# A decoder's second layer: gate logits by seven half-block products for eight, one weight unit a group

## The reference, cut to what matters

```python
h = _modulate(x, norm1[l], sh1, sc1)
q_a, k_a, v_a, q_b, k_b, v_b, q_n, k_n, v_n, gate_l = jnp.split(h @ w_in[l], IN_OFFSETS, axis=-1)
...
def _merge(outs, gate_logits, w_branch, w_out):
    g = jax.nn.sigmoid(gate_logits.astype(jnp.float32)).astype(gate_logits.dtype)
    g = g.reshape(*g.shape[:-1], N_BRANCHES, D_MODEL)
    y = g[..., 0, :] * (outs[0] @ w_branch[0])
    for n in range(1, N_BRANCHES):
        y = y + g[..., n, :] * (outs[n] @ w_branch[n])
    return y @ w_out
...
x = x + g1 * _merge((o_a, o_b, o_n), gate_l, w_branch[l], w_out[l])
```

## Time and profile before

| | us |
|---|---|
| runs | 1591.43, 1591.34, 1588.87 (median 1591.34) |
| profiled execution | 1588.37 |
| its span, first to last instruction | 1586.7 |
| PE busy | 1533.8 (97%) |
| PEld busy | 832.6 (52%) |
| DVE busy | 700.8 (44%) |
| ACT busy | 365.5 (23%) |
| POOL busy | 129.7 (8%) |

### The profile page before, as it was taken

How to read it: one execution, slowest core, us unless ns; L and a number is a source line. 1 busy time by engine, 2 the same in 40 slices (tenths; PEclk the granted TensorE clock), 3 DMA queues, 4 the chain that set the end, 5 groups by cost and what they waited for, 6 DMA issues and landing times.

```text
span 1586.7 us, 17758 instructions
## 1 busy us (share of the span) xinstructions
PE 1533.8 (97%) x6722; PEld 832.6 (52%) x6722; DVE 700.8 (44%) x1492; ACT 365.5 (23%) x868; POOL 129.7 (8%) x203
## 2 busy tenths in 40 slices
PE   8999999999999999999999989999999999989897
PEld 4478766667776646544444434446654445333332
DVE  2455378699985345311111145305776227111113
ACT  3022288711111111111011023106820011000001
POOL 1100001100000100000100020000300000101010
PEclk9999999999999999999999999999999998999999
DMA  9722320134744462689999696443159766999997
GB/s 333 268 67 94 107 80 16 27 119 138 277 161 176 156 251 107 226 310 401 406 413 401 273 351 207 143 169 93 41 155 367 270 246 253 386 407 412 414 366 286
DMA packets 109622, 371.81 MB, mean 234 GB/s; under 512 B 25136, under 2 KB 29376, under 8 KB 93060
## 3 DMA queue, kind: packets, MB, share of 16 engines
q1 hardware_dynamic: 96688, 332.42, 56.7%
q0 software_dynamic: 12416, 37.95, 6.7%
q10 hardware_dynamic: 432, 0.29, 0.1%
HBM read 362.55 MB, written 19.73 MB: 241 GB/s over the span
## 4 chain that ended last, share of the span: by engine, by line
PE 87%; DMA 8%; DVE 3%; ACT 1%; issue 1%; SPq 0%; POOL 0%; POOLq 0%; DVEq 0%; ACTq 0%
PE bank L2559 9%; PE bank L2459 7%; PE bank L2507 6%; PE bank L2861 6%; PE bank L2540 5%; DMA ring_sb<-w_e_down 5%; PE bank L2746 5%; PE bank L2840 5%; PE bank L2849 5%; PE bank L2568 5%; PE bank L2879 4%; PE bank L2885 4%; PE bank L2601 4%; PE bank L2611 4%; PE bank L2582 4%; PE bank L2456 3%
## 5 line engine op out<-in xcount | busy, mean ns | idle before, releaser
L2861 PE MATMUL bank<-ring_sb,HT_sb 128*64 128x512 f32 x544 | 122.1, 601 | 1.1 <-ACT HT_sb L1370 0.7
L2459 PE MATMUL bank<-ring_sb,HT_sb 128*128 128x512 f32 x256 | 114.9, 605 | 2.5 <-ACT HT_sb L1106 2.5
L1489 DVE SCALAR_TENSOR_TENSOR MB_sb<-ring_sb,cT_sb,MB_sb 128x512 f32<-128x512 f32 x144 | 108.3, 752 | 5.1
L2885 PE MATMUL bank<-ring_sb,QR_sb 128*64 128x512 f32 x336 | 81.8, 631 | 17.4 <-DMA ring_sb<-w_e_down 14.9
L2540 PE MATMUL bank<-ring_sb,HT_sb 128*128 128x512 f32 x192 | 85.4, 595 | 2.0 <-issue 2.0
L2568 PE MATMUL bank<-QR_sb,ring_sb 128*128 128x512 f32 x192 | 86.3, 592 | 0.0
L2145 DVE TENSOR_TENSOR QR_sb<-QR_sb,bank 64x512 f32<-64x512 f32 x21 | 21.9, 1043 | 139.1 <-ACT QR_sb L1380 139.1
L2459 PEld LDWEIGHTS bank<-ring_sb,HT_sb 128*128 128x128 f32 x256 | 48.9, 194 | 63.1 <-issue 63.1
L2879 PE MATMUL bank<-ring_sb,QR_sb 128*128 128x512 f32 x176 | 77.9, 595 | 0.8 <-DMA ring_sb<-w_e_down 0.8
L2861 PEld LDWEIGHTS bank<-ring_sb,HT_sb 128*64 128x64 f32 x544 | 38.9, 138 | 72.9 <-issue 71.7
L2582 PEld LDWEIGHTS bank<-tab_sb,MB_sb 128*128 128x128 f32 x480 | 51.4, 141 | 43.8 <-issue 41.3
(11 more groups left out here) (426 smaller groups left out, 2388.5 us busy)
## 6 DMA issues: line engine op xcount, KB each, us to landing
ring_sb<-w_e_down SPq DMA_DIRECT2D x32, 2048.0 KB, 14.6
ring_sb<-w_mod SPq DMA_DIRECT2D x24, 2048.0 KB, 10.7
ring_sb<-w_in SPq DMA_DIRECT2D x21, 2048.0 KB, 16.4
ring_sb<-w_e_gate SPq DMA_DIRECT2D x16, 2048.0 KB, 11.2
ring_sb<-w_e_up SPq DMA_DIRECT2D x16, 2048.0 KB, 12.4
ring_sb<-w_e_gate SPq DMA_DIRECT2D x22, 1024.0 KB, 17.4
ring_sb<-w_e_up SPq DMA_DIRECT2D x22, 1024.0 KB, 18.5
ring_sb<-w_branch SPq DMA_DIRECT2D x8, 1024.0 KB, 13.7
```

What stands on the lines that cost most here:

```text
L2459: ins = mm(bank[j % 4][:, :], HT[:, k, P * t:P * t + P], WR[slot][:, k], start=(k == 0), stop=(k == KD - 1))
L2861: ins = mm(bank[0][HALF * side:HALF * side + HALF, :], hgT[q % 2][:, k, 0:HALF], w[k], start=(k == 0), stop=(k == KD - 1))
L2885: ins = mm(bank[4][HALF * half:HALF * half + HALF, :], eaT[:, k, 0:HALF], w[k][:, CW * half:CW * half + CW], start=(k == 0), stop=(k == 3))
```

## The change

The second layer's gates take the form of the first. A group is now one weight unit of 512 columns and both token tiles, so there are six groups, 12 to 17 (`ALL_GATES`); their blocks are 512 inputs by 256 columns of weights, and 128 tokens by 512 inputs. The tokens stand still and the weights move, four 128x256 matmuls a product. Tile 1 is the first block row, so that tile 0's gates are whole first. The weight sums go into the context halves of the query buffers (S2, S3, and the copy of P5) and into the working buffer (S4), the token sums into the context half of the normalised tokens. The modulation blocks, which belonged to the steps 0 to 7, belong to the steps 0, 1, 2, 4, 5, 6, 8 and 9 (`mod_step`), each issued a step ahead, and the modulation rows follow them. The slots of the ring are dealt out anew. The diff has first the functions, then ScalarE's program, VectorE's and TensorE's.

```diff
+def mod_step(l, i):
+    return i + i // 3 if l else i
...
         def gate_weights(g):
 
-            w, r = WR[landed[f"g{g // 4}{g // 2 % 2}", 0][0]], g % 2
-            return [[w[:, KH * j:KH * (j + 1), HW * i + P * r:HW * i + P * r + P] for j in range(2)] for i in range(2)]
...
+            w = WR[landed[unit_of(g)][0]]
+            first, n = (0, HW) if g >= GATE_GROUPS else (P * (g % 2), P)
+            return [[w[:, KH * j:KH * (j + 1), HW * i + first:HW * i + first + n] for j in range(2)] for i in range(2)]
+
+        later = slice(SEQ, CW)
...
+                    {"S3": qT[B][:, :, later], "S2": qT[N][:, :, later],
+                     "S4": WK[:, D:2 * D].rearrange("p (k n) -> p k n", k=KH)}]
+        gate_third = [WK[:, D + CW:D + CW + HW], qT[A][:, 2, later]]
...
+                for g in gate_groups(l):
+                    if g > gate_groups(l)[0]:
+                        eng.wait_ge(merged, 2 * g if l else 2 * g - 1)
+                        keep_gate(g, sg[l][:, 0:HW], "X", "P1")
                         eng.wait_ge(whole, gate_joins(g, 0))
-                    keep_gate(g, gate_third, "Y", "P5")
+                    keep_gate(g, gate_third[l], "Y", "P5")
+                    if l:
+                        keep_gate(g, sg[0][:, 0:HW], "X", "P6")
+                        keep_gate(g, sg[0][:, HW:CW], "X", "P7")
+                        eng.wait_ge(whole, gate_joins(g, 3))
+                        act(sg[0], sg[0], ACT.Sigmoid).then_inc(part_kept, 1)
+                        act(sg[1][:, 0:HW], sg[1][:, 0:HW], ACT.Sigmoid)
+                        eng.wait_ge(product_mm, gate_no(g, "P4"))
+                        act(sg[1][:, HW:CW], gate_at["X"], ACT.Sigmoid).then_inc(part_kept, 1)
+                        continue
...
-                for i in range(len(merge_jobs(l)) if l else 0):
-                    eng.wait_ge(gate_mm, i + 1)
-                    eng.wait_ge(merged, before(merge_jobs, l) + i - 1)
-                    act(sg[i % 2], bank[i % 2][:, :], ACT.Sigmoid).then_inc(sig_ready, 1)
...
                 for s in range(M + 2):
-                    if l == 0 and s == M:
-                        gate_sum_1(0)
+                    if l and s in (6, 9, 12, 15):
+                        second_token_sum((s - 6) // 3)
+                    if s == M:
+                        gate_sum_1(gate_groups(l)[0])
...
-                    if i + 1 < halves:
-                        half_mod(l, i + 1)
+                    for m in range(1, halves):
+                        if mod_step(l, m) == i + 1:
+                            half_mod(l, m)
...
+                    g, second = divmod(i, 2)
+                    if second == 0:
+                        gate_join(g)
+                        if g + 1 in gate_groups(l):
+                            gate_sum_1(g + 1)
+                            gate_sum_2(g + 1)
+                            gate_sum_4(g + 1)
+                    eng.wait_ge(part_kept, gate_kept_no(g, "second" if second else "first"))
...
+                    g, second = divmod(i, 2)
+                    for name in GATE_PRODUCTS[6:] if second else GATE_PRODUCTS[4 if g == gate_groups(l)[0] else 0:6]:
+                        gate(g, name)
+                    if i >= 2:
                         eng.wait_ge(merged, i - 1)
-                        for k in range(KD):
-                            ins = gate_product(bank[i % 2], wg, k, t)
-                        ins.then_inc(gate_mm, 1)
```

More of the change, by code:

```diff
@@ L172, with gate_groups, unit_of @@
 GATE_GROUPS = 2 * 2 * NB
+ALL_GATES = GATE_GROUPS + 2 * NB
+def gate_groups(l):
+    return range(GATE_GROUPS, ALL_GATES) if l else range(GATE_GROUPS)
+def unit_of(g):
+    if g < GATE_GROUPS:
+        return f"g{g // 4}{g // 2 % 2}", 0
+    return f"g{(g - GATE_GROUPS) // 2}{(g - GATE_GROUPS) % 2}", 1
 def gate_no(g, name):
@@ L232, in rows_at @@
     first, count = next(x for x in sum_groups(l) if x[0] <= end < x[0] + x[1])
-    return first + count + sum(first <= b[3] < end for b in late_mods(l))
+    ahead = sum(first <= b[3] < end for b in late_mods(l))
+    return mod_step(l, first + count - 1) + 1 + (ahead // 2 if l else ahead)
 def stored(l, j):
@@ L292, in unit_uses @@
             for t in queries(l):
-                uses += [(("mod", lm, j), 1000 + end) for lm, j, first, end in late_mods(l) if max(first - 1, 0) == i]
+                uses += [(("mod", lm, j), 1000 + mod_step(l, end)) for lm, j, first, end in late_mods(l)
+                         if max(mod_step(l, first) - 1, 0) == i]
                 uses += [(("mod", lm, j), 1000 + at) for lm, j, at in whole_mods(l) if at - 2 == i]
@@ L2618, in _ @@
                             eng.wait_ge(exp_done, 2 * (M0 + M))
[L2619 to L2627 removed]
+                        gate(gate_groups(l)[0], GATE_PRODUCTS[s - M])
                 eng.wait_ge(o_copied, (M0 + M) // (H // 2))
@@ L2687, in _ @@
                     for g, (first, count) in enumerate(sum_groups(l)):
-                        if first + count - 1 == done:
+                        if mod_step(l, first + count - 1) == done:
                             row_sums(g)
```

110 lines of the change are left out of this document (46 added, 64 removed).

## The result

Fifteen executions of the changed kernel have a median of 1594.32 us (1588.36 to 1600.45), fifteen of the kernel before 1590.49 (1586.47 to 1593.38). The ratio is 1.0031, with a 95% interval of 1.0021 to 1.0041: 4.9 us slower, 3.3 to 6.5. The forecast was 2.3 us slower. The main case held, with its two large terms; it was too small by 2 us, in attention, in the sizes of the waits and in the clock. By the forecast's own measure of 0.2% this is slower, to which it gave 0.32, and not the same, to which it gave 0.56. That the time of 1593.6 us was missed by only 0.7 us is partly luck: the forecast stood on a median of 1591.34 for the kernel before, which came out at 1590.49.

The account below looks back on a forecast made before the run. TensorE was taken as the bound (87% of the chain): 9.9 + 1.96 - 0.75 - 10.8 = 0.3 us gained, less 2.6 for the clock, 2.3 slower, 1593.6 us on the median; range for 8 in 10, 1588 to 1598.

Parts of the forecast that it names:

- The main case: Second layer's merge: product savings nearly eaten by new waits, plus a low clock; 2.3 us slower, 1593.6 us, chance 0.48.
- The saving per product: Second-layer gates on TensorE: seven products at 1.73, 12.09 for 13.74 us; 1.65 saved a group, 9.9 for six.
- The hole of 1.96 us: TensorE's one idle time in the second layer's merge; claimed to go if weights come in time, 1.96 us gained.
- The waits: TensorE idle in the merge, ahead of P1 once and later groups' P6: 1.8 + 5.8 + 1.8 + 1.4 = 10.8 us.
- The clock: After the 5.8 us wait TensorE's clock falls to 1.2 GHz, costing 2.6 us on P6, P3, P7; bounds 0 and 2.8.
- Attention's end: Two weight sums ahead of the last two normalisations delay TensorE's transposes; 0.75 us lost, bounds 0.3 and 1.2.
- The token sums: Four VectorE sums, 0.7 us each, in the attention steps' 0.83 us gap; costed at nothing, 2.8 without that cover.
- A: Rival: the same waits in the merge but the clock stays up; 0.3 us gained, 1591.0 us; chance 0.22.
- B: Rival: VectorE keeps up in the merge and the copy finds its merge done; 11.1 us saved, 1580.2; chance 0.10.
- C: Rival: the merge's weights come late, 3 us more idle on TensorE; 5.3 us slower, 1596.6 us; chance 0.20.
- my own sign for C: In the merge: VectorE's first sum of a group waits for a transfer, which would show that weights come late.
- The tail: Behind the merge: residual gate loads issued at 1287, landing near 1294, within 1297; nothing counted for the late loads.

Follow-up runs that it names:

- e5_before_late_blocks: Kernel before with only the change's order of second-layer modulation blocks, their loads and rows, gates unchanged; ratio 0.9996 to the kernel before.
- e1_own_place: Changed kernel with ScalarE keeping second-layer product P1 in a place of its own, its copy not waiting for the previous group's second merge; ratio 0.9948 to before.
- e3_clock_kept: Changed kernel plus twelve unused 128x256 matmuls on TensorE in the 5.78 us wait ahead of the second group's P6; ratio 1.0013 to before.
- e4_attention_sums: Changed kernel with token sums moved to attention steps 5 to 8 and the first group's first two weight sums behind the last normalisations; ratio 1.0014 to before.
- e11_best: e7_all_parts with first weight sums in halves in attention, second modulation block later, branch weights awaited only at the branch product; 1580.86 us, ratio 0.9946 to before.
- e2_block_later: Changed kernel with the third modulation block behind the first group's second merge instead of between its two merges; ratio 1.0017 to before.
- e7_all_parts: Changed kernel with the edits of e1_own_place and e4_attention_sums, and the third gate unit issued ahead of the branch weights; ratio 0.9969 to before.
- e8_all_blocks_early: e7_all_parts with the modulation blocks at steps 0, 1, 2, 3, 4, 6, 7, 8; ratio 1.0005 to before.
- e10_fill_selection: e1_own_place with two more filling 128x512 matmuls on TensorE ahead of the second layer's selection; ratio 0.9974 to before.

## Why the prediction was right, and where not

**The saving per product** was right to the row: 1.73 us from start to start, seven in 12.09, with the weight loads hidden.

The prediction's first paragraph has a slip: the stretch from 1163.87 on holds 11 gate products and not 12 (the first is in attention), and 120.7 us is the sum with 11. The saving counts all 12 rightly.

**The hole of 1.96 us** went, as forecast, but through the order of loads (e5_before_late_blocks), not the products, and it was only 1.26 us in before's second profile.

**The waits** were right in place, number, order and releaser. By the idle times shown they are 1.57, 5.78, 1.96 and 1.14, together 10.45, where I had 1.8, 5.8, 1.8 and 1.4. From start to start they take TensorE 11.3 us (1.73, 6.02, 2.21, 1.38): each also costs some 0.2 us (0.16 to 0.25) that the idle time in the profile leaves out. The step that P6 waits for ScalarE's copy, and this for the second merge, is shown by e1_own_place, which cut it there and got 10.7 us back.

**The clock** fell where I had it, for 3.02 us and not 2.6, above my bounds (0 and 2.8). e3_clock_kept shows that the wait is the cause and that the low clock's price is real on the spot. It also shows what my sum did not say: the price is not a term that can be given back by itself. Where a later round is VectorE's, 2.5 of 2.9 us turn into a longer wait and a low clock behind it. So "what does the clock cost" has the answer 3.0 in the timeline and 0.4 in the stretch.

**Attention's end** was mis-sized: 0.95 against 0.75, inside the bounds.

**The token sums** are the step that failed: "They fall into the gap that VectorE has in an attention step ... I cost them at nothing." The gap I had read, 0.83 us, is that of a step without a mask, and the sums stood in others too: in step 9, the change to masked steps, 0.23 us was left over, and in step 15 GpSimd's additions stretched sum and normalisations, 0.66. Together 0.89, between my 0 and the 2.8 without cover. e4_attention_sums moved them and got 0.86 back in attention, of which 0.4 is left in the whole stretch.

These make the difference: 1.1 us in attention, 0.5 in the waits, 0.4 in the clock; 2.3 + 2.0 = 4.3, what the profile has in this stretch.

**Rivals.** A is refuted by the clock's row. B (11.1 us gained) did not happen, but it describes e1_own_place and e11_best, 8.3 and 8.6 us faster than before: VectorE's 100 us of work do fit into the stage if TensorE isn't tied to its order in one place. C had next to no price in the changed kernel. For the third group's unit VectorE was later still; for the fourth group's its first sum did wait, which was my own sign for C, in the round that ends in the wait of 1.96 us:

```profile
1220.16 1.23 DVE L1571 TENSOR_TENSOR QR_sb<-ring_sb 128x1024 f32<-128x1024 f32 x1 [0.36 <-DMA ring_sb<-w_in]
```

And the third group's unit was nearer to being late than I had it. The time from issue to landing, 18.5 us in my sum, was 18.4 in e1_own_place and 18.7 in e2_block_later; the issue was at 1179.37 and not at 1177, so by my estimate it landed near 1198. In e2_block_later that was the bound.

**The tail.** The residual gate was issued at 1290.54 and not at 1287, took 14 us beside the experts' loads and not some 7, and landed at 1304.5, not 1294 to 1297. The normalisation's rows behind it, which my sum left out, landed at 1316.74. The conclusion, nothing at the end, was right within 0.3 us, and this was luck: the output products did cover the late gate, as I had it, but the rows that I had not counted came only during the fourth and last of these products.

**Open.** For e7_all_parts, e8_all_blocks_early and e10_fill_selection the ratio is 2.8, 3.7 and 2.4 us worse than their profile in attention and merge, while for the change itself and all the others it fits within the interval. Against the second profile of before it is 0.7 less each, which puts e10_fill_selection inside its interval and leaves the other two outside. The part behind the merge differs by 4.5 us between profiles and by 2.6 between two of one kernel; one profile of each can't say whether a kernel's mean is shifted there.

## What to carry to other kernels

When products take the place of an operand in a buffer that is still waiting to be merged, follow each copy to the merge that frees its place: a wait there holds TensorE, and the engines behind it, for a reason that the arithmetic doesn't show; a place of its own, 1 KB in each partition, was worth 10.7 us here. A stage with two nearly full engines gives back little of what is gained at one place, so find the next wait in line before pricing the first. And a gap between steps has to be read in the very steps in which the new work will stand.

## What the runs showed that I had not expected

A wait of 1.96 us left the clock up (changed kernel, ahead of the fourth group's P6: the granted clock stayed at 1.00), one of 2.04 (e4_attention_sums) was followed by two products of 2.33 and 2.89 us from start to start for 1.73, and one of 2.92 (e3_clock_kept) by 3.08 and 2.14; after 5.78 us of idling the low clock lasted through two products in one kernel and through one in another:

```profile
1190.01 3.56 PE L2602 MATMUL bank<-QR_sb,HT_sb 128*128 128x256 f32 x8 [5.78 <-ACT WK_sb L1235]
1193.41 1.89 PE L2602 MATMUL bank<-WK_sb,HT_sb 128*128 128x256 f32 x8
...
1232.96 2.54 PE L2602 MATMUL bank<-QR_sb,HT_sb 128*128 128x256 f32 x8 [2.04 <-ACT WK_sb L1235]
1235.29 3.05 PE L2602 MATMUL bank<-WK_sb,HT_sb 128*128 128x256 f32 x8
```

With e2_block_later's, which cost 1.9 behind 5.83 us, the price of a wait of this length was 3.0, 1.9 and 1.7 us in three kernels, so my one estimate of 2.6 stood for a spread. The other surprise is the 25 us for 2 MB of the normalisation's rows on GpSimd's queue, behind 1 MB of the gate's and beside six loads of 1 MB on SyncE's that were issued from 1290.3 to 1293.2. The DMA engines moved 370 GB/s on the mean from 1291.6 to 1316.8, which is the 9 MB and little else; I had counted 1 MB of each side.
